# Even mixer: carry by heads, silu from the tangent, values copied earlier, pairs weighed a step later, divisors by logarithm

## What is computed

```python
proj = rms_norm_2(x, mix_norm) @ w_in
q, k, v, z, xbc, dt_raw = jnp.split(proj, EVEN_SPLITS, axis=-1)
na_out = neighbourhood_attention(q, k, v, na_rel_bias)      # 8 heads of 64, softmax over a window
xs, bm, cm = jnp.split(jax.nn.silu(centred_depthwise_conv(xbc, conv_w, conv_b)), ...)
y = y_fwd + y_bwd + D_skip[:, None] * xs                    # chunked scans, 16 heads, 4 chunks of 128
def step(h, inp):                                           # the carry between chunks
    s_c, d_c = inp
    return h * d_c[..., None, None] + s_c, h
# gated_group_rms_norm: 4 groups of 256
h = (y * jax.nn.silu(z)).reshape(Bsz, S, SSD_GROUPS, Dn // SSD_GROUPS)
h = h * lax.rsqrt(jnp.mean(h * h, axis=-1, keepdims=True) + NORM_EPS)
return jnp.concatenate([na_out, ssd_out], axis=-1) @ w_out
```

## Time and profile before

| what | us |
|---|---|
| median of 3 runs (2907.25, 2907.39, 2893.02) | 2907.25 |
| the profiled execution's own time | 2909.55 |
| its span | 2907.7 |
| TensorE busy | 2779.8 (96%) |
| VectorE busy | 1527.9 (53%) |
| ScalarE busy | 1059.4 (36%) |
| GpSimd busy | 779.3 (27%) |

### The profile page before, as it was taken

One profiled execution on the slowest core, in us unless ns is written; L12 is line 12 of the kernel. 1 busy time (PEld: TensorE's weight loads), 2 busy tenths in 40 slices (PEclk: granted clock), 3 DMA queues, 4 the chain that ended last, 5 costly groups with the idle time before them and its releaser, 6 DMA issues. The chain is left out here.

```text
span 2907.7 us, 37500 instructions
## 1 busy us (share of the span) xinstructions
PE 2779.8 (96%) x13734; PEld 2211.1 (76%) x13734; DVE 1527.9 (53%) x1889; ACT 1059.4 (36%) x1868; POOL 779.3 (27%) x710
## 2 busy tenths in 40 slices
PE   8999999799899999999999888899999999999999
PEld 6888888557798778888677766588888756788887
DVE  4477762644643577774467555653433346644432
ACT  5333332334333433333255445422222247422221
POOL 3231112440812531112102535221111135411100
PEclk9999999899898999999999889999999999999999
DMA  4222233211100023223222021132233310122333
GB/s 148 79 95 94 95 91 96 89 44 58 52 1 19 1 88 100 94 91 95 85 87 80 15 61 43 39 104 95 94 93 95 100 53 1 58 94 94 101 86 103
DMA packets 80539, 218.96 MB, mean 75 GB/s; under 512 B 21917, under 2 KB 22045, under 8 KB 80158
## 3 DMA queue, kind: packets, MB, share of 16 engines
q1 hardware_dynamic: 79262, 215.17, 23.8%
q10 hardware_dynamic: 1152, 2.10, 0.2%
HBM read 215.14 MB, written 2.10 MB: 75 GB/s over the span
## 5 line engine op out<-in xcount | busy, mean ns | idle before, releaser
L311 PE MATMUL psum<-rounded,high_r 128*128 128x512 f32 x3040 | 1205.5, 397 | 45.6 <-PEq L120 11.0
L313 PE MATMUL psum<-rounded,high_r 128*128 128x512 f32 x3040 | 1191.2, 392 | 0.0
L315 PE MATMUL psum<-rounded,ring_low 128*128 128x512 f32 x3040 | 1190.4, 392 | 0.0
L331 ACT ACTIVATE high_r<-ring 128x1024 fp32r<-128x1024 f32 (+2 forms) x432 | 420.4, 973 | 1409.3 <-PE psum L315 1388.8
L336 DVE TENSOR_TENSOR ring_low<-ring,high_r 128x1024 fp32r<-128x1024 f32 (+2 forms) x430 | 526.8, 1225 | 566.1 <-ACT high_r L331 564.8
L311 PEld LDWEIGHTS psum<-rounded,high_r 128*128 128x128 f32 x3040 | 575.9, 189 | 203.4 <-issue 48.2
L315 PEld LDWEIGHTS psum<-rounded,ring_low 128*128 128x128 f32 x3040 | 575.5, 189 | 121.9
L313 PEld LDWEIGHTS psum<-rounded,high_r 128*128 128x128 f32 x3040 | 576.3, 190 | 118.5 <-issue 1.4
L769 DVE TENSOR_TENSOR arena<-psum,inverse 128x512 f32<-128x512 f32 x176 | 121.5, 691 | 314.3 <-PE psum L315 314.2
L624 POOL CAST rounded<-rows 128x512 f32 (+1 forms) x88 | 53.9, 613 | 785.4 <-DVE rows L774 785.4
L626 POOL TENSOR_TENSOR rounded<-rows,rounded 128x512 f32 (+1 forms) x88 | 115.6, 1313 | 13.2 <-POOL rounded L624 11.9
(11 more groups left out here) (413 smaller groups left out, 2985.7 us busy)
## 6 DMA issues: line engine op xcount, KB each, us to landing
ring<-in_up SPq DMA_DIRECT2D x176, 512.0 KB, 3.3
ring<-in_down SPq DMA_DIRECT2D x64, 384.0 KB, 3.1
ring<-in_down SPq DMA_DIRECT2D x64, 320.0 KB, 2.9
ring<-in_even_in SPq DMA_DIRECT2D x36, 512.0 KB, 3.7
ring<-in_sgu_in SPq DMA_DIRECT2D x16, 512.0 KB, 3.5
ring<-in_even_out SPq DMA_DIRECT2D x16, 384.0 KB, 3.1
ring<-in_qkv SPq DMA_DIRECT2D x12, 512.0 KB, 3.7
ring<-in_sgu_out SPq DMA_DIRECT2D x8, 512.0 KB, 3.3
```

The source lines that it names most:

```text
L311: nc.tensor.matmul(psum[:, m, :], high_r[:, r % HIGHS, blk], x_high, start=(k0 + k == 0), stop=False)
L313: nc.tensor.matmul(psum[:, m, :], high_r[:, r % HIGHS, blk], x_low, start=False, stop=False)
L315: mm = nc.tensor.matmul(psum[:, m, :], ring_low[:, r % R, blk], x_high, start=False, stop=end)
L331: nc.scalar.activation(high_r[:, r % HIGHS, 0:nk * P], ring[:, r % R, 0:nk * P], ACT.Copy).then_inc(unit_high, 1)
```

## The change

Six edits in the even mixer. (1) The carry: eight instructions, one for each direction and head, multiply the old state by that head's decay and add the new state from PSUM; the wait for `state_done` now stands ahead of them. (2) `spread` and `argue` of units 0 and 1 go from step 23 to step 22. (3) `keep_values` for tiles 0, 1 goes from after unit 29 to after unit 28, ahead of step 0; for tiles 2, 3 from after unit 30 to after unit 29, ahead of step 1. (4) silu(z) = z (1 + tanh(z/2)) / 2: ScalarE computes the tangent, VectorE one more instruction z (1 + t); the factor 2 that is left drops out in the group norm, with 4e-6 in place of 1e-6. (5) The first weighing of pairs 1, 2, 3 is done a step later. (6) The group norm's divisors are exp(-ln(.)/2) on ScalarE, all eight tiles at once after step 18; the spreads and norms follow in a row, the last four spreads inside `even_out`, and the low parts of odd tiles are taken by GpSimd.

The diff, cut to its core:

```diff
+                        if i in (9, 13):
+                            weigh_values(i - 5)
...
-                        if i >= 4:
...
+                        if i >= 4 and (i % 4 or i == 4):
+                            weigh_values(i - 4)
...
                     def spread_gated(i):
-                        pe.wait_ge(gate_inverted, 2 if i >= 6 else 1)
                         if i == 0:
+                            pe.wait_ge(gate_inverted, 1)
...
-                        if n == VALUES - 1:
+                        if n == VALUES - 2:
                             spread(0)
                             spread(1)
+                        if n == VALUES - 1:
                             products_bc(0)
                             spread(2)
...
                         if i == 16:
-                            pe.wait_ge(gate_guarded, 1)
                             gather_gated(6)
                             gather_gated(7)
-                            spread_gated(0)
-                        if i > 16:
-                            for k in range(2 * i - 33, min(2 * i - 31, 6)):
-                                spread_gated(k)
+                            weigh_values(12)
+                    for k in range(4):
+                        spread_gated(k)
...
                         if n > GATES and n % 2:
                             for z in (n - 1, n):
                                 act.wait_ge(scaled, z + 1)
-                                nc.scalar.activation(home(z), home(z), ACT.Silu).then_inc(silu_done, 1)
+                                if z < GATES + 2:
+                                    act.wait_ge(brought_scaled, HEADS)
+                                else:
+                                    act.wait_ge(silu_done, 16 + z - GATES - 1)
+                                nc.scalar.activation(normed_tile[z % 2], home(z), ACT.Tanh, scale=0.5).then_inc(tanh_done, 1)
...
-                    def root(ps):
-                        act.wait_ge(gate_guarded, 1 if ps is GROUPS_FIRST else 2)
-                        nc.scalar.activation(gate_roots[ps], rows[ps, 0, :], ACT.Sqrt).then_inc(gate_rooted, 1)
+                    def gate_divisors():
+
+                        act.wait_ge(gate_gathered, KD)
+                        nc.scalar.activation(rows[:, 0, :], psum[:, 6, :], ACT.Ln, bias=con("eps", 1, 1), scale=1.0 / 256).then_inc(gate_rooted, 1)
+                        act.wait_ge(gate_rooted, 1)
+                        nc.scalar.activation(rows[:, 0, :], rows[:, 0, :], ACT.Exp, scale=-0.5).then_inc(gate_inverted, 1)
...
-                        if n == VALUES - 1:
+                        if n == VALUES - 2:
                             argue(0)
                             argue(1)
+                        if n == VALUES - 1:
...
-                        if GATES < n <= GATES + 2:
-                            keep_values(2 * (n - GATES) - 2)
-                            keep_values(2 * (n - GATES) - 1)
                         if n >= GATES:
                             for k, i in enumerate(steps_behind(n)):
+                                if n <= GATES + 1 and k == 0:
+                                    keep_values(2 * (n - GATES))
+                                    keep_values(2 * (n - GATES) + 1)
                                 step(i)
...
-                        if i == 15:
-                            root(GROUPS_FIRST)
                         if i == 18:
-                            root(GROUP_LAST)
-                        if i > 16:
-                            for k in range(2 * i - 34, min(2 * i - 32, 6)):
-                                gated_high(k)
+                            gate_divisors()
                     out_of(PAIRS - 1)
-                    gated_high(6)
-                    gated_high(7)
+                    for i in range(KD):
+                        gated_high(i)
...
+                            dve.wait_ge(state_done, 3 * grp + k + 1)
                             for back in range(2):
-                                nc.vector.tensor_tensor(by_head(new, back, back + 1), by_head(old, back, back + 1),
-                                                        heads_of(OVER, 3 - k if back else k, grp, back, back + 1),
-                                                        ALU.mult).then_inc(decayed, 1)
-                            dve.wait_ge(decayed, 4 * grp + 2 * k)
-                            dve.wait_ge(state_done, 3 * grp + k + 1)
-                            nc.vector.tensor_tensor(new, psum[:, 4 + k % 2, :], new, ALU.add).then_inc(state_kept, 1)
+                                for h in range(4):
+                                    at = slice(back * GW + h * HD, back * GW + (h + 1) * HD)
+                                    d = (3 - k if back else k) * 32 + back * 16 + 4 * grp + h
+                                    last = nc.vector.scalar_tensor_tensor(out=new[:, at], in0=old[:, at], scalar=OVER[:, d:d + 1],
+                                                                          in1=psum[:, 4 + k % 2, at], op0=ALU.mult, op1=ALU.add)
+                            last.then_inc(state_kept, 1)
...
                     def low(i):
+                        if i % 2:
+                            return
                         dve.wait_ge(gate_high, i + 1)
-                        nc.vector.tensor_tensor(rounded(Z)[:, i, :], normed_tile[i % 2], rounded(XT)[:, i, :].bitcast(F32), ALU.subtract).then_inc(gate_low, 1)
+                        nc.vector.tensor_tensor(rounded(Z)[:, i, :], normed_tile[0], rounded(XT)[:, i, :].bitcast(F32), ALU.subtract).then_inc(gate_low, 1)
 
                     def normed_of(i):
                         dve.wait_ge(gate_spread, i + 1)
                         if i >= 2:
                             low(i - 2)
-                            dve.wait_ge(gate_low, i - 1)
+                            dve.wait_ge(gate_low_pool if i % 2 else gate_low, i // 2)
                         nc.vector.scalar_tensor_tensor(out=normed_tile[i % 2], in0=arena[:, Z + i, :], scalar=col("ssd_g", i), in1=psum[:, (5, 7)[i % 2], :],
                                                        op0=ALU.mult, op1=ALU.mult).then_inc(gate_normed, 1)
 
                     def gate(j):
+
+                        dve.wait_ge(tanh_done, j + 1)
+                        x = arena[:, Z + j, :]
+                        nc.vector.scalar_tensor_tensor(out=x, in0=normed_tile[j % 2], scalar=1.0, in1=x, op0=ALU.add, op1=ALU.mult).then_inc(silu_done, 1)
                         dve.wait_ge(y_turned, j + 1)
                         dve.wait_ge(silu_done, 16 + j + 1)
...
                     out_of(PAIRS - 1)
-                    normed_of(6)
-                    normed_of(7)
+                    for i in range(KD):
+                        normed_of(i)
                     low(6)
-                    low(7)
...
+                    for i in range(1, KD, 2):
+                        pool.wait_ge(gate_high, i + 1)
+                        nc.gpsimd.tensor_tensor(rounded(Z)[:, i, :], normed_tile[1], rounded(XT)[:, i, :].bitcast(F32),
+                                                ALU.subtract).then_inc(gate_low_pool, 1)
+
             def even_out_ready(pe):
                 def ready(k):
-                    if k in (6, 7):
+                    if 4 <= k < 8:
                         later[0](k)
                     if k < 4:
                         pe.wait_ge(out_low, k + 1)
                     else:
-                        pe.wait_ge(gate_low, k - 3)
+                        pe.wait_ge(gate_low_pool if k % 2 else gate_low, (k - 2) // 2)
```

51 lines of the change are left out of this document (16 added, 35 removed).

## The result

The changed kernel takes 2892.39 us (median of 20, 2881.33 to 2897.07) where the kernel before takes 2908.68 (median of 20 on the same chip, 2893.02 to 2911.94). The ratio is 0.9946, 95% interval 0.9935 to 0.9957: 16.3 us less, 2891.5 forecast.

A forecast was written before the change was run, and what follows sets the result against it. The prediction took idle TensorE (45 of 285 us) and its clock between two levels as the bound. Terms 0.5 + 3.8 + 6.8 + 0 + 4.4 gave 15.5 us, so 2891.5 from a median of 2907.25; range 2874 to 2902.

The forecast's parts named there:

- Pairs argued earlier: Scan: TensorE's 2.38 us wait for the third spread goes, but only 0.5 us is passed on; bounds 0 and 2.4.
- The carry by heads: Scan: eight short instructions per carry save VectorE 4.0 us; gain taken as 3.8, bounds a loss of 0.2, VectorE gain 12.4.
- Contention with GpSimd: VectorE beside GpSimd: contention only with GpSimd's two-tensor work; head instructions near 0.27 us and gate instruction 0.69 not stretched.
- Values ahead and tangent: Attention, unit 29's end to unit 30's start: about 11.7 us becomes 4.9, gain 6.8; 5.5 the price if nothing covers gates.
- The 6.8 carries on: Attention: the 6.8 us gained by unit 30 passes through steps 3 to 7, all shifted alike.
- Pairs weighed later: Attention, steps 8 to 16: gains of 1.2 and 1.0 us against 2.2 lost; net 0, bounds -2 and +4.
- The -2.2 for a low spell behind step 10: Attention: a new wait of some 2.8 us at step 10 puts following matmuls at the low clock, costing 2.2.
- The tail: Tile 6's turn to first output tile's end: 42.0 us becomes 36.1, gain 5.9, less 1.5 for low-clock spreads: 4.4.
- Rival 1: Whole stretch: low-clock spells vanish with the gaps, 10 us more gain, 2881; chance 0.17.
- Rival 2: Scan and attention: gate instructions held by GpSimd's normalisations and heads unoverlapped, gain only 7.5, 2900; chance 0.22.
- Rival 3: Scan and steps re-form behind POOL's windows, nothing passed on, 2907; chance 0.05.
- Rival 4: Step 6 to tail's end: TensorE stays at the low clock, about 42 us added, 2933; chance 0.06.

The follow-up runs named there:

- e8: Changed kernel with silu back on ScalarE in place of the tangent, values still copied ahead; 2892.1 us, ratio 0.9944 to the kernel before.
- e12: The changed kernel run again unaltered, for a second profile; 2893.8 us, ratio 0.9931 to the kernel before.
- e4: e3 with the first four spreads placed among the first output tile's products; 2886.7 us, ratio 0.9927 to the kernel before.
- e6: Changed kernel with every pair weighed at its own step, no weighing deferred; 2890.2 us, ratio 0.9931 to the kernel before.
- e3: Changed kernel with ScalarE's logarithm and exponential for the divisors moved ahead of step 17's copy; 2884.3 us, ratio 0.9917 to the kernel before.
- e9: e3 with all low parts on VectorE, none on GpSimd; 2890.6 us, ratio 0.9939 to the kernel before.

## Why the prediction was right in sum and wrong in its terms

- **Pairs argued earlier, 0.5.** Measured 1, within the scatter. Right in kind: the 2.38 goes, and the first `inside` waits 1.2 instead (forecast 1.3).
- **The carry by heads, 3.8.** The step that failed is "VectorE gains 4.0 ... I take 3.8". VectorE did gain 4.0, and each instruction cost what I worked out. But TensorE lost 5.1 us of waits, and 4.8 us more because the matmuls behind these waits had run at 1.2 GHz: 9.6 to 10. I credited the low level where the values' wait goes and charged it behind new waits, but in this term it stood at nothing, without a reason. The bound of 12.4 was VectorE's time; what I said TensorE's waits allow, about 8, was passed.
- **Contention with GpSimd.** Right for the kernel: 272 and 682 ns, not stretched. The Trainium skill, SBUF — State Buffer, section Who interferes with whom, has a VectorE instruction with two SBUF inputs contend with one of GpSimd that reads SBUF. The trace agrees that they meet, but it is GpSimd that is held: the pair of normalisations beside `L336` and `L2840` takes 4.37, not 3.10. GpSimd waits 2.26 us behind that pair, so its 1.27 lay on no path. The 0.37 by which the next pair is longer did lie on it: step 6's scores wait 0.36 more in the first profile than in e8.
- **Values ahead and tangent, 6.8.** The attention is 7.5 shorter in the first profile and as much in e12 and e4 to 0.3 us, but 2.8 to 4.1 in the five other executions of the same code. The gain up to unit 30 is as summed. What failed is "The 6.8 carries on", with "less some 0.4 for the gate's instruction": of it 3.8 us were waits (4.15 and 1.39 for 1.75), and over the whole stage TensorE's waits fall from 16.6 to 15.9, or to 14.3 in e12. In e8, without the gate's instruction, they fall to 12.7, by 3.9. So the copies passed on the 3.8 (the deferral moves nothing, by e6), and the gate's instruction cost 1.6 to 3.2 where 0.4 to 0.8 was charged. That 7.5 came out is the clock's doing, and luck.
- **Pairs weighed later, net 0.** Right within what can be told. The waits moved from the low parts to the scores (2.73 and 2.26 at steps 10 and 14). The -2.2 for a low spell behind step 10 was right in some executions and wrong in others, see below.
- **The tail, 36.1 and a gain of 4.4 after the clock.** The first part of the sum was right: to the first spread 18.8 us forecast, 19.0 in e12 (20.4 in the first profile, where the gathers ahead ran slow too). The step that failed is the second part, 17.3 with "one or two spreads may run at the low level ... minus 1.5": it takes 21.0 in e12, 3.7 over, and 23.6 in the first profile. The low level held a part of the four spreads and the first six to eight products, and in the first profile a second spell came at 1841, 15 us behind the last wait of any length. TensorE is busy 34.6 to 38.6 us, before 32.3, and the tail is 40.0 to 44.0. With the wait gone (e3, e9) it is 36.3 and 36.2. That this is the forecast's bare sum is chance, since 36.1 had the wait in it.
- **Rival 1** (low spells vanish) was right in part: 4.8 us in the scan, and 2.3 to 6.8 in the attention (busy 96.9 to 92.4, before 99.2). **Rival 2**: the gate's instruction is not stretched (0.68), nor are the heads, so its mechanism did not show; that gates lie on TensorE's path did, by another way (e8). **Rival 3** (nothing passed on) did not show in the scan; in the attention the waits came back within 0.7 us of what they were. **Rival 4** had the right place, the tail, and a small part of its price.

The sum, 15.5 for 16.3, was luck: two errors of 6 us that cancelled in the first profile, and in a typical one a scan 6 better than forecast against an attention up to 4 worse and a tail 2 to 4 worse. That the tail is 3.6 us or more shorter without its wait is shown by e3 and e9. That the wait brings on the low level is argued: e3 and e4, without it, have low-level matmuls there too (granted clock 0.95 and 0.91). Why the low level takes 4 us more in one execution is not settled, and I made no experiment on it.

## What to carry to other kernels

On a chain where TensorE waits again and again, price a removed wait at up to twice its length (5.1 us of waits gave 10 in the scan), since the matmuls behind it may leave the low level too; price an added wait the same way, in each term. Compare idle and busy time of a stage, not its length alone: two kernels of 108.2 and 108.3 us differed by 3 us of waits and 3 of clock. Look for an engine's idle piece ahead of the last dependency before shortening the operation: the divisors' new form gained about 2 us of tail behind step 18 and 4 or more on top of it two copies earlier. When two edits cure the same wait, try each alone, as e8 did: one of the two here cost waits.

## What the runs showed of the hardware

**The same wait, two clocks.** Step 10's scores in the changed kernel (above, 1770.40) and in e3, whose code is the same up to there:

```profile
1761.94 2.08 PE L2388 MATMUL psum<-arena 64*128 64x512 f32 x4 [2.73 <-DVE work L2807]
```

A wait of 2.73 us is followed by 1.13 at the high level in one and by 2.08 at the low one in the other; e3's attention is 4.5 us longer for such spells, with all waits equal (13.6, 1.9 and 0.4). The Trainium skill, TensorE: Matmul & The Clock Gate, Part 1, says of the start of a kernel that how many matmuls run slow differs from run to run. These rows show the same in its middle. It is also what moves the untouched stages. From 760 us to the last tap, e3 and then e12:

```profile
760.00:1574.40 814.40, 791.75 (x4503) 663.04 (x4504) 478.12 (x618) 309.53 (x693) 219.09 (x223) 0.98 0.21 67
```

```profile
760.00:1589.10 829.10, 805.77 (x4503) 676.78 (x4504) 479.19 (x620) 309.65 (x693) 220.21 (x224) 0.97 0.21 66
```

The same 4503 matmuls are busy 14.0 us less in e3, and the idle time differs by 0.7. That is of the size by which executions of one kernel scatter here.

**A table load costs 1.28 us and no more** in these rows. In e3 the load starts at 1810.06 and its activation at 1811.36, right behind. A logarithm and an exponential next to each other took two loads, not one.
